# One norm chain for the final norm and the first norm of the second model, and the first row block ahead at both of its layers' beginnings

## The reference

```python
x = x + (gate * ffn).astype(x.dtype)          # end of the MoE layer
x = rmsnorm(x, final_norm)                    # x / sqrt(mean(x^2) + 1e-6) * final_norm
# second model, twice:
shift, scale, gate = split(silu(c) @ w_ada + b_ada)
h = rms_norm(x, pre_g) * (1 + scale) + shift
proj = h @ w_in                               # 1024 -> 4096
...                                           # rope, two kinds of attention, gates
y = rms_norm(concat @ w_out, post_g)
x = x + gate * y
```

## Time and profile before

| | us |
|---|---|
| median of 3 runs | 2113.41 |
| the 3 runs | 2116.64, 2106.52, 2113.41 |
| the profiled execution: its time | 2106.99 |
| the profiled execution: its span, first to last instruction | 2105.2 |

### The profile page before, as it was taken

How to read it: one execution, slowest core, us unless ns; L and a number is a source line. 1 busy time by engine, 2 the same in 40 slices (tenths; PEclk the granted TensorE clock), 3 DMA queues, 4 the chain that set the end, 5 groups by cost and what they waited for, 6 DMA issues and landing times.

```text
span 2105.2 us, 28640 instructions
## 1 busy us (share of the span) xinstructions
PE 2002.7 (95%) x10428; PEld 1659.3 (79%) x10428; DVE 1717.4 (82%) x2424; ACT 1322.4 (63%) x1973; POOL 0.2 (0%) x4
## 2 busy tenths in 40 slices
PE   6998999998989999999999999999999999999997
PEld 5777899978877788888888888888888866777776
DVE  7688878768777698989899898998989987886764
ACT  4354534355564688778787777778778774545543
POOL 0000000000000000000000000000000000000000
PEclk9999999999999999999999999999999999999999
DMA  9846688846332399999999898999999984672630
GB/s 375 292 148 204 238 311 317 293 141 205 125 104 96 107 375 339 357 327 365 356 354 355 326 367 325 377 349 340 365 318 370 364 336 149 222 230 80 210 111 20
DMA packets 154212, 560.20 MB, mean 266 GB/s; under 512 B 17233, under 2 KB 17489, under 8 KB 153937
## 3 DMA queue, kind: packets, MB, share of 16 engines
q1 hardware_dynamic: 154064, 558.29, 73.3%
HBM read 557.18 MB, written 1.05 MB: 265 GB/s over the span
## 4 chain that ended last, share of the span: by engine, by line
PE 76%; DVE 14%; ACT 6%; issue 3%; DMA 1%; DVEq 0%; SPq 0%; ACTq 0%
PE ps L526 21%; PE ps L528 20%; PE ps L527 20%; PE ps L532 11%; DVE spl L515 6%; PE ps L536 3%; ACT sph L503 2%; DVE macc L579 2%; DMA ring<-in_mod 1%; ACT arena L2089 1%; DMA ring<-in_dense_down 1%; ACT arena L758 1%; DVE arena L2123 0%; ACT ps L849 0%; DVE hL L843 0%
## 5 line engine op out<-in xcount | busy, mean ns | idle before, releaser
L515 DVE TENSOR_TENSOR spl<-ring,sph 128x1024 fp32r<-128x1024 f32 x906 | 1077.8, 1219 | 280.2 <-ACT sph L503 271.3
L503 ACT ACTIVATE sph<-ring 128x1024 fp32r<-128x1024 f32 x906 | 949.1, 1058 | 552.3 <-PE ps L528 421.4
L526 PE MATMUL ps<-sph,hH 128*128 128x512 f32 (+1 forms) x1296 | 519.9, 401 | 3.8 <-DVE hL L843 3.8
L528 PE MATMUL ps<-sph,hL 128*128 128x512 f32 (+1 forms) x1296 | 507.2, 391 | 0.0
L527 PE MATMUL ps<-spl,hH 128*128 128x512 f32 (+1 forms) x1296 | 506.1, 391 | 0.0
L526 PEld LDWEIGHTS ps<-sph,hH 128*128 128x128 f32 x1296 | 245.4, 189 | 53.5 <-issue 5.7
L528 PEld LDWEIGHTS ps<-sph,hL 128*128 128x128 f32 x1296 | 244.9, 189 | 52.5
L527 PEld LDWEIGHTS ps<-spl,hH 128*128 128x128 f32 x1296 | 245.7, 190 | 47.8 <-issue 0.7
L526 PE MATMUL ps<-sph,rH 128*128 128x512 f32 x664 | 269.9, 406 | 5.3 <-ACT arena L3034 1.7
L528 PE MATMUL ps<-sph,rL 128*128 128x512 f32 x664 | 260.7, 393 | 0.0
L527 PE MATMUL ps<-spl,rH 128*128 128x512 f32 x664 | 260.3, 392 | 0.0
(11 more groups left out here) (305 smaller groups left out, 1760.1 us busy)
## 6 DMA issues: line engine op xcount, KB each, us to landing
ring<-in_moe_gu SPq DMA_DIRECT2D x448, 512.0 KB, 5.3
ring<-in_moe_down SPq DMA_DIRECT2D x224, 512.0 KB, 5.3
ring<-in_mod SPq DMA_DIRECT2D x144, 512.0 KB, 4.9
ring<-in_w_in SPq DMA_DIRECT2D x64, 512.0 KB, 4.4
ring<-in_dense_gu SPq DMA_DIRECT2D x44, 512.0 KB, 5.3
ring<-in_ssm_w_in SPq DMA_DIRECT2D x40, 512.0 KB, 3.5
ring<-in_dense_down SPq DMA_DIRECT2D x22, 512.0 KB, 5.4
ring<-in_hyb_w_in SPq DMA_DIRECT2D x20, 512.0 KB, 5.9
```

The costliest lines, as they stand in the source:

```text
L503: a.activation(k.high[m % SPLITS][:, 0:w], raw[:, 0:w], ACT.Copy).then_inc(k.S.half_rounded, 1)
L515: v.tensor_tensor(k.low[m % SPLITS][:, 0:w], raw[:, 0:w], k.high[m % SPLITS][:, 0:w], ALU.subtract).then_inc(*k.tick(k.S.half_split, f"hal ...
L526: pe.matmul(out, a[0], b[0], start=start, stop=False, skip_group_check=True)
L528: return pe.matmul(out, a[1], b[0], start=False, stop=stop, skip_group_check=True)
```

## The change

For the join of the models, the final norm and norm 4 get their roots from one chain. DVE first multiplies `X` by the final norm's weights into a space of its own (L2927, four halves); ACT squares `X` (as before) and these weighted halves (L2907). With m the mean square of `X` plus 1e-6 and w the sum of squares of the weighted halves over 1024 plus m times 1e-6, the norm of the final norm's result is the weighted half over the root of w, so one root of w for each block gives `xn` for norm 4 (L2948). The final norm's own result, which the layer needs at its end, is written to `X` later (`final_rows_scalar`, `final_rows_vector`, L2960), behind norm 4. For both layers, PE transposes block 0 only, runs fillers, runs the first piece's products of block 0, and then transposes block 1 (`norm_turn_tensor`). The fillers become 4 and 3 for norm 4, and 3 and 6 for norm 5. At the second join, DVE's and ACT's instructions of norm 5 are put between those of block 1's output, one of the two weight pieces is split later, and norm 5's `norm_fill` of block 0 stands ahead of the root of block 1.

```diff
-NORM_FILL = (0, 6, 6, 6, 11, 7)
+NORM_FILL = (0, 6, 6, 6, 4, 3)
...
     if i > 3:
         fill(pe, k, banks, NORM_FILL[i])
-    for t in range(NT):
...
+    for t in range(NT - 1 if i > 3 else NT):
+        norm_turn_tensor(pe, k, i, t, banks)
...
+    if i > 3:
+        fill(pe, k, banks, 6 if i == 5 else 3)
...
@@ def norm_scalar(a, k, i):
-    for t in range(NT if i > 3 else 0):
-        norm_root_scalar(a, k, i, t)
+    if i == 5:
+        norm_root_scalar(a, k, 5, 1)
+        for h in range(2):
+            norm_round_scalar(a, k, 5, 0, h)
+        norm_fill_scalar(a, k, 5, 1)
+        for h in range(2):
+            norm_round_scalar(a, k, 5, 1, h)
+        return
...
@@ def norm_vector(v, k, i, before):
+    if i == 5:
+        norm_mean_vector(v, k, 5, 1, before)
+        norm_newton_vector(v, k, 5, 1)
+        for h in range(2):
+            norm_low_vector(v, k, 5, 0, h)
+        norm_scale_vector(v, k, 5, 1)
+        split_vector(v, k, k.stream.first["second_out0"] + 5 + SPLITS)
+        norm_fill_vector(v, k, 5, 1)
+        for h in range(2):
+            norm_low_vector(v, k, 5, 1, h)
+        return
...
-    for t in range(NT):
-        norm_fill_vector(v, k, i, t)
-        for h in range(2):
-            norm_low_vector(v, k, i, t, h)
+    norm_fill_vector(v, k, 4, 0)
+    newton_vector(v, k, "n4.1", k.st[:, 43:44], k.st[:, 41:42], k.st[:, 45:46])
+    for h in range(2):
+        norm_low_vector(v, k, 4, 0, h)
+    final_scale_vector(v, k, 1)
+    norm_fill_vector(v, k, 4, 1)
+    for h in range(2):
+        norm_low_vector(v, k, 4, 1, h)
...
 def final_scalar(a, k):
...
     for t in range(NT):
         for c in range(2):
-            a.wait_ge(*k.when(f"final.x{2 * t + c}"))
-            square(a, k, "final", t, c, k.final_space[:, 2 * t + c, :])
+            a.wait_ge(*k.when(f"sc{N_EXP - 1}.{t}.added{c}"))
+            square(a, k, "moe", t, c, k.E.acc[:, t, c * 512:(c + 1) * 512])
+        if t == 1:
+            root_scalar(a, k, "n4.0", k.st[:, 44:45], k.st[:, 40:41])
+        for c in range(2):
+            n = 2 * t + c
+            a.wait_ge(*k.when(f"final.weighted{n}"))
+            a.wait_ge(*k.when(f"moe.squared{n}"))
+            a.activation(k.E.acc[:, t, c * 512:(c + 1) * 512], k.final_space[:, n, :], ACT.Square,
+                         accum_out=k.st[:, 48 + n:49 + n]).then_inc(*k.tick(k.S.squared, f"final.squared{n}"))
+    root_scalar(a, k, "n4.1", k.st[:, 45:46], k.st[:, 41:42])
...
 def final_vector(v, k):
...
+    v.wait_ge(*when("fnorm.copied4"))
+    for t in range(NT):
+        for c in range(2):
+            n, s = 2 * t + c, slice(c * 512, (c + 1) * 512)
+            v.wait_ge(*when(f"sc{N_EXP - 1}.{t}.added{c}"))
+            v.tensor_tensor(k.final_space[:, n, :], k.X[:, t, s], k.macc[:, s], ALU.mult).then_inc(*tick(S.weighted, f"final.weighted{n}"))
...
+def final_scale_vector(v, k, t):
+    for c in range(2):
+        n, s = 2 * t + c, slice(c * 512, (c + 1) * 512)
+        v.tensor_scalar(k.norm_space.xn[:, t, s], k.final_space[:, n, :], k.st[:, 42 + t:43 + t], None,
+                        ALU.mult).then_inc(*k.tick(k.S.norm_scaled, f"n4.x{t}"))
+
+
+def final_rows_vector(v, k):
...
+    newton_vector(v, k, "final", y, m, t0)
+    for t in range(NT):
         for c in range(2):
-            s = slice(c * 512, (c + 1) * 512)
-            v.scalar_tensor_tensor(out=k.X[:, t, s], in0=k.X[:, t, s], scalar=y, in1=k.macc[:, s], op0=ALU.mult,
-                                   op1=ALU.mult).then_inc(*tick(S.added, f"final.x{2 * t + c}"))
+            n, s = 2 * t + c, slice(c * 512, (c + 1) * 512)
+            v.tensor_scalar(k.X[:, t, s], k.final_space[:, n, :], k.st[:, 36 + t:37 + t], None, ALU.mult).then_inc(*tick(S.added, f"final.x{n}"))
...
@@ def second_tensor(pe, k, l):
                         if t == 1:
                             last.then_inc(k.S.half_used, 1)
+                        elif q == 0:
+                            norm_turn_tensor(pe, k, 4 + l, 1, turns)
...
+def second_out_vector(v, k, l, m):
...
+    second_root_vector(v, k, l, 0)
+    for c in range(2):
+        second_gated_vector(v, k, l, 0, c)
+    for c in range(2):
+        second_added_vector(v, k, l, 0, c)
+    if l == 0:
+        split_vector(v, k, m + 4 + SPLITS)
+    second_root_vector(v, k, l, 1)
+    second_gated_vector(v, k, l, 1, 0)
+    if l == 0:
+        norm_mean_vector(v, k, 5, 0, "s0")
+    second_gated_vector(v, k, l, 1, 1)
+    if l == 0:
+        norm_newton_vector(v, k, 5, 0)
+        norm_scale_vector(v, k, 5, 0)
+    for c in range(2):
+        second_added_vector(v, k, l, 1, c)
+    if l == 0:
+        back_until(v, k, "vector", 5, "sum")
+        v.wait_ge(*k.when("mod5.ready"))
+        norm_fill_vector(v, k, 5, 0)
```

113 lines of the change are left out of this document (68 added, 45 removed).

## The result

| | before | after |
|---|---|---|
| median of 20 runs each, us | 2114.7 | 2108.55 |
| lowest and highest | 2106.52, 2120.14 | 2102.89, 2117.79 |
| the profiled execution: its time | 2106.99 | 2110.27 |
| its span, and mean clock | 2105.2, 0.984 | 2108.5, 0.982 |

The ratio of the times is 0.9975, with a 95% interval of 0.9965 to 0.9984: 5.3 us less, between 3.4 and 7.4 (the plain difference of the two medians is 6.2). The forecast was 0.22% less. The interval lies clear of 1, but the gain is under the half per cent that I had called "no change".

A forecast was written before the change was run, and what follows sets the result against it. PE was taken as the bound (76% of the chain), so time comes only where it lacks real work. First join -4.3 us (-3.7 + 1.1 - 1.7) and second -0.4 sum to -4.7: 2108.7 us, range 2101 to 2116.

The forecast's parts named there:

- DVE past its branch, behind the last add: First join: DVE's new multiplies start at 1736.9 us, bounds 1734.6 and 1737.6.
- `xn` to the first product: First join: from block 0's `xn` at 1742.4 through transposes, fill, Newton step and lows to the product at 1747.6.
- first join, to the product: First product of the second model's layer 0 comes 3.7 us earlier, 1747.6 instead of 1751.28.
- second join, to the product: One weight piece less ahead of block 1's root; first product 1.5 us earlier, at 1933.4.
- block 1's transposes, each join: Now behind the first six products, they add 1.1 us of PE time that stood in a gap before.
- clock behind the first product: First join: the slow stretch from 1752.7 to 1756.1 goes as fillers fill the gap; 1.7 us won, bounds 0 and 1.7.
- The new chain: First join: weighted halves 1736.9 to 1739.4, then small steps, root, Newton and scales; `xn` at 1742.4, 3.5 us earlier.
- No new wait: First join: block 1's `xn` is made by 1748.0, before the six products end at 1749.0, so PE does not wait.
- A: Rival: half the gain, slow stretch stays somewhere and DVE's branch costs its full 3.02 us; -2.3 us, 2111.1; chance 0.22.
- B: Rival: fillers at the low clock delay the first products at both joins; +3.5 us, 2116.9; chance 0.08.
- C: Rival: DVE past its branch at 1734.6, fillers no bound; -6 us, 2107.4; chance 0.58 together with the forecast.
- D: Rival: nothing PE waits for moves; block 1's low part or weight piece late, 4 us back; -0.5 us, 2112.9; chance 0.12.

The follow-up runs named there:

- no_fill: Changed kernel without the fillers between block 0's transposes and the first product (three and six): 2111.89 us in one execution; timed again, ratio 0.9982.
- before_again: The kernel before, with no edit, profiled a second time: 2113.09 us.
- second_only: Kernel before with the change at the second join only, first join left as before: ratio 0.9987.
- joint_only: Changed kernel with one chain for both norms, but both blocks' transposes ahead at norm 4 in the old order: 2112.05 us.
- first_only: Kernel before with the change at the first join only, second join left as before: ratio 0.9985.
- newton_first: Changed kernel with block 1's Newton step of norm 4 ahead of DVE's fill, and 5 fillers instead of 6 at norm 5: ratio 0.9971.
- no_branch: Changed kernel without the path for overfull experts and the branch around it on all engines: 2111.20 us.
- early: Changed kernel with the four weighted halves made ahead of DVE's branch, right behind its adds: 2109.03 us.

## Why the prediction was right

Time in us. The forecast of 0.22% less met a measured 0.25% (0.16 to 0.35).

| step | forecast | measured |
|---|---|---|
| DVE past its branch, behind the last add | 2.3 | 2.13 in after; 1.17 to 2.65 over all profiles |
| from there to `xn` of block 0 | 5.5 | 5.32 |
| `xn` to the first product | 5.2 | 5.12 |
| first join, to the product | -3.7 | -4.15 |
| second join, to the product | -1.5 | -1.92 |
| block 1's transposes, each join | +1.1 | +0.9 at the first, +1.2 at the second |
| clock behind the first product | -1.7 | not shown, not excluded |
| sum | -4.7 | -4.0 without the clock; -5.3 (-3.4 to -7.4) by the runs |

- *The new chain.* Right in each link. The two scales of 512 columns, for which there was no row, took 0.88 together (0.8 taken, between 0.75 and 1.5). The weighted halves took 2.50 (2.5). The first join came out 0.45 above the forecast, of which the branch is 0.2, the rest the faster links.
- *The second join.* Forecast 12.98 us, measured 12.56. I had both ends, the low parts and the six fillers, at 1933.4 on before's time line. `no_fill` shows that the low parts alone give 12.37, 0.6 us earlier than I had worked out. The fillers ended nearer to what I had: the second matmul is 13.19 us behind the sums, which is 12.88 for a product that starts unhindered.
- *The transposes.* Charged at their length in a row of a gap, 1.09. They cost 0.9 at the first join, and 1.2 at the second (0.9 and the 0.3 of the sixth filler).
- *No new wait.* DVE's fill of block 1 waited 2.00 us for PE and PE never for `hL` of block 1 in after; the late writing of `X` lies in what was idle time. Right.
- *The clock.* This is the weak step of the sum. I read one low stretch in one execution as a property of the join. It is only half one. Over all profiles, a join in the old form with its idle time behind the short transposes had a clock under 1 behind the product in 4 of 7 cases (table: first join of before, before_again, second_only and joint_only; second join of before, before_again and first_only), in the new form with fillers in 0 of 17, and without fillers in 4 of 4. So the new form does hold the clock there. But the profiles of L0 show no time saved by it: the low clock cost 5.1, 5.1, 5.1 and 6.8 us in the four with the old first join, and 6.8, 5.1, 3.4, 5.1, 5.1, 5.1, 6.8 and 6.8 in the eight with the new one and its fillers. The low stretches are as many and stand elsewhere in the layer. The mean clocks of the timed executions can't decide it: 0.9816 over the 20 of after, 0.9807 and 0.9806 over two series of 23 of before, timed apart from them. The difference, 0.0010 with 0.0011 of noise either way, would be 1.4 us by the slope above, and may be nothing. So the 1.7 us stood on one profile; it is neither shown nor excluded. The Trainium skill, "TensorE: Matmul & The Clock Gate", section "What's actually happening", has the low clock as the default and activity as what releases it. The traces agree at the joins: behind the first products the clock was 1.00 in 17 of 17 cases with fillers and under 1 in 4 of 4 without.

That the total still came out right is partly luck: the -1.7 from the clock had one profile behind it, and the joins gave 0.9 us more than forecast, which made up for half of it. The transposes took 0.1 less.

The rivals. A (half the gain) rested on the low stretch staying somewhere, which L0 shows, and on a branch of 3.02 us, which DVE never showed; the measured gain excludes -2.3 us. B (slower by fillers at the low clock) did half happen, and in the kernel before more than after: its eleven fillers lost up to 1.4 us (before_again). In after and `newton_first` the four ahead of the transposes ran at the low clock and made these at most 0.46 us late; those in front of a product took 0.44 to 0.46 us for each of their two matmuls, the full rate. C (-6, DVE past its branch at once) is within the interval of the ratio, but its mechanism is excluded: the branch costs 1.6 to 2.3 us (`no_branch`). D (a wait of block 1 eats the gain; 4 us back from -4.7 are -0.7, not the -0.5 that I wrote) is excluded by the stretches: L0 grew by 0.9 and L1 by 1.2 to 1.4, and no more.

What stays open: the joins and the transposes make -4.0 us by the first profiles and -5.5 by the second ones (14.32 - 20.04 - 1.91 + 2.1), -4.8 on the mean of both (0.2 less with the 1.4 of the whole L1), and the runs -5.3. Of the second -5.5, 1.4 are old fillers at the low clock. So the chains alone can account for the gain, within the interval of the runs; what part of it came through the clock, at the joins and in the layers, was not settled.

## What to carry to other kernels

Where an element-wise scale and two norms follow each other, take the sum of squares of the weighted input beside the plain one and do both roots from it: here one chain in place of three was 3 us, while starting one row block ahead earned 0.3 to 0.7 us and cost 0.9 in transposes that no gap hides any more. Such an order pays only where it wins more ahead of the first product than the operations cost that it moves out of a gap. Fillers should be counted at the low clock as well: a row of them that just fits into a gap at the full clock is late at the low one. And a low clock seen at one place of one execution isn't a term for a sum: take a second execution, or the whole layer's clock, first.

## What the hardware showed that was not expected

- *The scatter goes with the clock.* Over the 20 runs of after, time and mean granted clock go together with a correlation of -0.94: 1.8 us less for each 0.001 of clock, from 2117.79 at 0.977 to 2102.89 at 0.984. In the six other timed series the correlation is -0.58 to -0.95. In the profiles the low clock comes mostly in stretches of 3.4 us at half speed, or twice that, and so costs 1.7 us a piece. They fall in dense products too, as here in after at 1781 and 1808:

```profile
1781.00:1785.00 4.00, 4.00 (x14) 3.29 (x14) 4.00 (x4) 0.60 (x1) 0.00 (x0) 0.57 0.71 244
1808.00:1812.00 4.00, 3.51 (x17) 3.51 (x18) 1.12 (x3) 2.15 (x3) 0.00 (x0) 0.58 0.60 202
```

- *They have their places.* Counted from the first product of layer 0, 11 of the 14 profiles have a low stretch 57 to 60 us behind it, and 13 have one of 6.8 us 135 to 139 us behind it (1885 to 1893 of the span). The one that has neither is the profile of before that the prediction was made from. Of the 13, nine had none at the second join, and eight of these had one near 1964 to 1971; the four with one at the second join (1933 to 1938) had none there. This is an observation on the profiles, and no run was made to explain it.
- *A branch that isn't taken into its path costs more than its instructions, and not the same each time.* Between DVE's last add and its next instruction were 1.17 to 2.65 us, for the same code 2.13 and 1.47 in two executions of after; PE showed 3.1 to 3.7 us, ACT 1.8 to 3.0 ahead of its table load. Without the branch DVE and ACT have none, and PE 1.25. A second stall of 2.02 us came two small instructions behind it in `early`, and none was seen where longer instructions stood there.
